# Two latent mixers reordered: rotation products first, keys copied by ScalarE, pooling products between the scores, rotary keys on 128 rows

## The reference

```
h = modulate(rms_norm(x, ffn1_norm[l]), sh1, sc1);  x = x + 0.5 * g1 * swiglu(h, ...)
h = modulate(rms_norm(x, mix_norm[l]), sh2, sc2)
z = h @ w_in[l]                       # 512 pooling, 384 query, 256 key/value, 64 rotary key
y_pool = (windowed means of z - z) @ pool_w[l], per group of 128, * pool_scale[l]
q = rms_norm(cq) @ w_q_b              # 4 heads of 128 plain + 64 rotary
k_nope, v = rms_norm(ckv) @ w_kv_b    # 4 heads of 128 and 128
q_rope, k_rope = apply_rope(...)      # x * cos + rotate_half(x) * sin; one k_rope for all heads
s = (q_nope . k_nope + q_rope . k_rope) * scale, causal, softmax over the keys, times v
x = x + g2 * (concat(y_pool, y_mla) @ w_out[l])
h = modulate(rms_norm(x, ffn2_norm[l]), sh3, sc3);  x = x + 0.5 * g3 * swiglu(h, ...)
```

## Time and profile before

| what | value |
|---|---|
| median of three executions | 1668.71 us (1668.25 to 1669.92) |
| profiled execution | 1669.04 us, of which the span is 1667.2 |
| mean granted TensorE clock | 0.985 |
| TensorE, its weight loads | 97% and 88% busy |
| VectorE, ScalarE, GpSimd | 76%, 51%, 4% busy |
| read from HBM | 340.6 MB, 205 GB/s |

### The profile page before, as it was taken

The page is one execution under the profiler, slowest core; times in us unless marked ns, Lnnn a source line. Parts: engine busy times, 40 slices in busy tenths (PEclk is TensorE's granted clock), DMA queues, the critical chain, the costliest instruction groups (busy, mean ns, idle before and its releaser), DMA issues.

```text
span 1667.2 us, 26979 instructions
## 1 busy us (share of the span) xinstructions
PE 1620.5 (97%) x11054; PEld 1461.2 (88%) x11054; DVE 1265.9 (76%) x1445; ACT 854.7 (51%) x1018; POOL 64.3 (4%) x77
## 2 busy tenths in 40 slices
PE   6999999999999999999999999999999999999997
PEld 6989999888689999899998799998899998799996
DVE  7967889877548897778878677885778887585554
ACT  4566555555256455554446464444544455454443
POOL 3001000000010000100000010000000000000000
PEclk8999999999799999999999999999999999999998
DMA  7514888654226986488874348975598844155550
GB/s 241 177 51 152 304 324 291 215 158 134 70 78 237 322 292 205 128 303 303 314 232 130 108 148 296 315 250 177 170 321 311 310 157 149 64 187 192 181 186 40
DMA packets 230974, 342.77 MB, mean 206 GB/s; under 512 B 7030, under 2 KB 194020, under 8 KB 230896
## 3 DMA queue, kind: packets, MB, share of 16 engines
q1 hardware_dynamic: 229888, 340.59, 60.3%
q0 software_dynamic: 704, 0.82, 0.2%
q10 hardware_dynamic: 304, 0.27, 0.1%
HBM read 340.60 MB, written 1.05 MB: 205 GB/s over the span
## 4 chain that ended last, share of the span: by engine, by line
PE 79%; DVE 11%; issue 5%; ACT 4%; POOL 0%; DMA 0%; DVEq 0%; ACTq 0%
PE PS L647 20%; PE PS L737 19%; PE PS L648 10%; PE PS L627 10%; PE PS L605 5%; DVE wl L1446 3%; PE PS L614 3%; PE PS L716 2%; PE PS L672 2%; ACT wh L1043 2%; PE PS L795 2%; PE PS L864 2%; DVE Z L1545 1%; PE PS L817 1%; DVE XL L1462 1%
## 5 line engine op out<-in xcount | busy, mean ns | idle before, releaser
L1446 DVE TENSOR_TENSOR wl<-raw,wh 128x2048 fp32r<-128x2048 f32 (+2 forms) x257 | 575.0, 2240 | 150.0 <-ACT wh L1043 147.9
L647 PE MATMUL PS<-HP,wh 128*128 128x512 f32 x1728 | 608.1, 395 | 0.2 <-DVE wl L1446 0.2
L1043 ACT ACTIVATE wh<-raw 128x2048 fp32r<-128x2048 f32 (+2 forms) x257 | 477.4, 1859 | 137.5 <-PE PS L737 117.9
L648 PE MATMUL PS<-HP,wl 128*128 128x256 f32 x1728 | 484.6, 280 | 0.0
L647 PEld LDWEIGHTS PS<-HP,wh 128*128 128x128 f32 x1728 | 324.0, 188 | 74.8 <-DVE wl L1446 0.5
L737 PE MATMUL PS<-FX,wh 128*128 128x256 f32 x1920 | 344.8, 281 | 1.9 <-DVE FX L1611 1.9
L648 PEld LDWEIGHTS PS<-HP,wl 128*128 128x128 f32 x1728 | 326.5, 189 | 0.0
L737 PEld LDWEIGHTS PS<-FX,wh 128*128 128x128 f32 x1920 | 294.5, 188 | 4.3 <-DVE wl L1446 2.1
L737 PE MATMUL PS<-FX,wl 128*128 128x256 f32 x960 | 269.9, 281 | 0.0
L737 PEld LDWEIGHTS PS<-FX,wl 128*128 128x128 f32 x960 | 180.4, 188 | 0.0
L1545 DVE SCALAR_TENSOR_TENSOR Z<-ada,CA,Z 128x1024 f32 x126 | 161.4, 1281 | 1.3
(11 more groups left out here) (263 smaller groups left out, 1796.9 us busy)
## 6 DMA issues: line engine op xcount, KB each, us to landing
ada<-ada_w SPq DMA_DIRECT2D x144, 512.0 KB, 6.3
raw<-ffn_w_gate SPq DMA_DIRECT2D x66, 1024.0 KB, 5.4
raw<-ffn_w_up SPq DMA_DIRECT2D x66, 1024.0 KB, 5.4
raw<-ffn_w_down SPq DMA_DIRECT2D x66, 1024.0 KB, 5.2
raw<-od_w_in SPq DMA_DIRECT2D x13, 1024.0 KB, 5.3
raw<-ev_w_in SPq DMA_DIRECT2D x10, 1024.0 KB, 7.9
raw<-w_in SPq DMA_DIRECT2D x8, 1024.0 KB, 5.5
raw<-w_out SPq DMA_DIRECT2D x8, 1024.0 KB, 6.1
```

What stands on the lines that cost most here:

```text
L647: mm(pairs(bank(bk)), lhsT=lhs(0, k), rhs=HP[:, k], start=k == 0, stop=False, skip_group_check=True)
L648: last = mm(bank(bk, 0, S), lhsT=lhs(1, k), rhs=HH[:, k, :], start=False, stop=k == k_tiles - 1, skip_group_check=True)
L1043: last = A_(dst(wh), src, ACT.Copy)
L1446: last = tt(dst(wl), src, dst(wh).bitcast(F32), ALU.subtract)
```

## The change

TensorE: the rotation group moves in front of `ada_turn` and the values' products, and `ada_turn` goes to bank 2. The pooling products move behind `scores(0)`, into banks 6 and 7. `spin(8)` and `spin(6, 6)` are left out, and the wait for `y_pool` moves behind `turn(1)`. VectorE: the rotary sums move in front of the adaptive columns; the rotary key is written into two tiles, KR with the key on partitions 0 to 63 and KX with it on 64 to 127, the other half of each zero, in place of one tile with the key doubled; the copy of the plain keys leaves VectorE; the pooling scale moves behind `masked(0)`, the `fill` behind `probs(0)`, and `lo(n0 + 10)` behind `masked(1)`. ScalarE: it gets the copy of the plain keys, in front of the values' copies, and `exps(0)` moves in front of the `fill`. GpSimd: it zeroes the other halves of KR and KX once the rotation group is through. The rotary scores now take all 128 partitions of the query tile, which holds two heads, against KR for even and KX for odd heads. The number of score products is the same.

```diff
@@ -417,8 +417,7 @@
                     half = slice(64 * (h % 2), 64 * (h % 2) + 64)
                     sc.append((h * w, [
                         (Z[:, ML["QN"] + h * S + b * P:][:, 0:P], Z[:, ML["KN"] + h * S:][:, 0:w]),
-                        (Z[half, ML["QR"] + (h // 2) * S + b * P:ML["QR"] + (h // 2) * S + (b + 1) * P],
-                         Z[half, ML["KR"]:ML["KR"] + w])]))
+                        (Z[:, ML["QR"] + (h // 2) * S + b * P:][:, 0:P], Z[:, ML[("KR", "KX")[h % 2]]:][:, 0:w])]))
                     va.append((bank((0, 3)[b], h * P, P),
                                [(Z[:, ML["V"] + kb * 512 + h * P:][:, 0:P], h * nk + kb) for kb in range(nk)]))
                 sc.sort(key=lambda e: (e[0] // w) % 2)
@@ -571,6 +570,12 @@
                         pool.tensor_tensor(sq[:, 2 * c, :], sq[:, 2 * c, :], sq[:, 2 * c + 1, :],
                                            ALU.add).then_inc(sq_sum, 1)
 
+            def zero_keys(l):
+
+                pool.wait_ge(ev("rot_full"), l + 1)
+                pool.memset(Z[64:P, ML["KR"]:ML["KR"] + S], 0.0).then_inc(ev("kr_zero"), 1)
+                pool.memset(Z[0:64, ML["KX"]:ML["KX"] + S], 0.0).then_inc(ev("kr_zero"), 1)
+
             for name in ("mix0", "ffn0", "mix1"):
                 add_squares(name)
             pool.wait_ge(ev("lru_gates"), 4)
@@ -579,9 +584,13 @@
             pool.dma_start(AR[0:12, 0:NSEL], const[0:12, NCONST:NCONST + NSEL]).then_inc(sel_in, 16)
             for name in ("ffn1", "fa0", "w0"):
                 add_squares(name)
+            zero_keys(0)
             pool.wait_ge(ev("pool_full"), 1)
             pool.dma_start(PW[:], A["pool_w_2"][1].rearrange("g c d -> c g d")).then_inc(aux_in[2], 16)
-            for name in ("fb0", "fa1", "w1", "fb1", "final"):
+            for name in ("fb0", "fa1", "w1"):
+                add_squares(name)
+            zero_keys(1)
+            for name in ("fb1", "final"):
                 add_squares(name)
 
         @block.tensor
@@ -972,41 +981,38 @@
                     last = product(bank(3 + h // 2, (h % 2) * S, S), lambda p, k: w(p, k, 256 * h, P),
                                    lambda p, k: H[p][:, 3 + k, :], 2)
                 last.then_inc(ev("kn_full"), 1)
-                ada_turn(f"w{l}", 6)
+                pe.wait_ge(ev("q_out"), 3 * l + 3)
+                mm(bank(6), lhsT=cn("rot"), rhs=Z[:, ML["QR"]:ML["QR"] + 512], start=True, stop=True)
+                mm(bank(0, 0, S), lhsT=cn("krdup", 64), rhs=Z[0:64, ML["KX"]:ML["KX"] + S], start=True, stop=True)
+                mm(bank(0, S, S), lhsT=cn("krrot", 64), rhs=Z[0:64, ML["KX"]:ML["KX"] + S], start=True,
+                   stop=True).then_inc(ev("rot_full"), 1)
+                ada_turn(f"w{l}", 2)
                 for b in range(NB):
                     last = product(bank(5 + 2 * b), lambda p, k: H[p][:, 3 + k, b * P:(b + 1) * P],
                                    lambda p, k: w(p, k, 0, 1024).rearrange("p (h c) -> p h c", c=256)[:, :, 128:256], 2)
                 last.then_inc(w_used, 1)
 
-                pe.wait_ge(ev("q_out"), 3 * l + 3)
-                pe.wait_ge(ada_out, ADA[f"w{l}"] + ADA_GAP[f"w{l}"])
-                mm(bank(6), lhsT=cn("rot"), rhs=Z[:, ML["QR"]:ML["QR"] + 512], start=True, stop=True)
-                mm(bank(0, 0, S), lhsT=cn("krdup", 64), rhs=Z[0:64, ML["KX"]:ML["KX"] + S], start=True, stop=True)
-                mm(bank(0, S, S), lhsT=cn("krrot", 64), rhs=Z[0:64, ML["KX"]:ML["KX"] + S], start=True,
-                   stop=True).then_inc(ev("rot_full"), 1)
-
+                rounds = latent_rounds()
+                scores, turn, values = attend("mla", l, rounds)
+                pe.wait_ge(ev("rope"), 2 * l + 2)
+                pe.wait_ge(ev("kn_out"), l + 1)
+                scores(0)
+                pe.wait_ge(ev("v_out"), 2 * l + 2)
                 pe.wait_ge(aux_in[1 + l], 16)
                 pe.wait_ge(ev("pool_diff"), 4 * l + 4)
                 for g in range(4):
-                    last = mm(bank(1 + g // 2, (g % 2) * S, S), lhsT=PW[:, g, :],
+                    last = mm(bank(6 + g // 2, (g % 2) * S, S), lhsT=PW[:, g, :],
                               rhs=cols(WK, 2176, 4)[:, g, :], start=True, stop=True)
                 last.then_inc(ev("pool_full"), 1)
-                rounds = latent_rounds()
-                scores, turn, values = attend("mla", l, rounds)
-                pe.wait_ge(ev("v_out"), 2 * l + 2)
-                spin(8)
-                pe.wait_ge(ev("rope"), l + 1)
-                pe.wait_ge(ev("kn_out"), l + 1)
+                pe.wait_ge(ada_out, ADA[f"w{l}"] + ADA_GAP[f"w{l}"])
                 n0, fill = U0[f"w_out{l}"], f"yw{l}"
-                scores(0)
-                spin(6, 6)
-                pe.wait_ge(ev("y_pool"), 4 * l + 4)
                 scores(1)
                 turn(0)
                 half_unit(n0, 4, fill, False)
                 values(0)
                 half_unit(n0 + 1, 5, fill, False)
                 turn(1)
+                pe.wait_ge(ev("y_pool"), 4 * l + 4)
                 spin(3, 7)
                 values(1)
                 half_unit(n0 + 2, 6, fill, False)
@@ -1395,6 +1401,8 @@
                 A_(Z[:, ML["QN"] + 512:ML["QN"] + 1024], bank(2), ACT.Copy).then_inc(ev("q_out"), 1)
                 A_(Z[:, ML["QR"]:ML["QR"] + 512], bank(1), ACT.Copy).then_inc(ev("q_out"), 1)
                 hi(nq + 4)
+                act.wait_ge(ev("kn_full"), l + 1)
+                A_(Z[:, ML["KN"]:ML["KN"] + 1024], banks(3, 2), ACT.Copy).then_inc(ev("kn_out"), 1)
                 act.wait_ge(w_used, nq + 3)
                 for b in range(NB):
                     A_(Z[:, ML["V"] + 512 * b:][:, 0:512], bank(5 + 2 * b), ACT.Copy).then_inc(ev("v_out"), 1)
@@ -1413,8 +1421,8 @@
                     else:
                         act.wait_ge(ev("mla_taken"), 2 * l + 2)
 
+                exps(0)
                 fill((0, 1), ready)
-                exps(0)
                 turned(0)
                 exps(1)
                 turned(1)
@@ -2013,32 +2021,27 @@
                         ALU.mult, ALU.subtract).then_inc(ev("pool_diff"), 1)
                 lo(n0 + 9)
 
-                ada_read(f"w{l}")
+                QR, t2 = Z[:, ML["QR"]:ML["QR"] + 512], WK[:, 0:512]
+                dve.wait_ge(ev("rot_full"), l + 1)
+                dve.wait_ge(ev("pool_diff"), 4 * l + 4)
+                dve.wait_ge(ev("tables"), 2)
+                own.mark(tt(pairs(t2), pairs(bank(6)), over(SIN[:], 2), ALU.mult))
+                own.mark(tt(pairs(QR), pairs(QR), over(COS[:], 2), ALU.mult))
+                own.mark(tt(WK[:, 512:768], bank(0, S, S), SIN[:], ALU.mult))
+                own.link(tt(WK[:, 768:1024], bank(0, 0, S), COS[:], ALU.mult))
+                own.mark(tt(QR, QR, t2, ALU.add))
+                dve.wait_ge(ev("kr_zero"), 2 * l + 2)
+                for h, name in ((0, "KR"), (64, "KX")):
+                    last = tt(Z[h:h + 64, ML[name]:ML[name] + S], WK[h:h + 64, 768:1024], WK[h:h + 64, 512:768], ALU.add)
+                    last.then_inc(ev("rope"), 1)
+
+                ada_read(f"w{l}", 2)
                 dve.wait_ge(ada_out, ADA[f"w{l}"] + ADA_GAP[f"w{l}"])
                 gain_cols(l, 2)
                 half_cols(l, 1)
                 shift_cols(1, 0 if l == 0 else 2)
                 if l == 0:
                     gain_cols(1, 0)
-
-                QR, t2 = Z[:, ML["QR"]:ML["QR"] + 512], WK[:, 0:512]
-                KR = Z[:, ML["KR"]:ML["KR"] + S]
-                dve.wait_ge(ev("rot_full"), l + 1)
-                dve.wait_ge(ev("pool_diff"), 4 * l + 4)
-                dve.wait_ge(ev("tables"), 2)
-                own.mark(tt(pairs(t2), pairs(bank(6)), over(SIN[:], 2), ALU.mult))
-                own.mark(tt(pairs(QR), pairs(QR), over(COS[:], 2), ALU.mult))
-                own.mark(tt(WK[:, 512:768], bank(0, S, S), SIN[:], ALU.mult))
-                own.link(tt(KR, bank(0, 0, S), COS[:], ALU.mult))
-                own.mark(tt(QR, QR, t2, ALU.add))
-                tt(KR, KR, WK[:, 512:768], ALU.add).then_inc(ev("rope"), 1)
-                dve.wait_ge(ev("kn_full"), l + 1)
-                dve.tensor_copy(Z[:, ML["KN"]:ML["KN"] + 1024], banks(3, 2)).then_inc(ev("kn_out"), 1)
-                lo(n0 + 10)
-                dve.wait_ge(ev("pool_full"), l + 1)
-                for g in range(4):
-                    last = ts(T[:, g, :], bank(1 + g // 2, (g % 2) * S, S), pc(f"ps{l}", g), None, ALU.mult)
-                    last.then_inc(ev("y_pool"), 1)
                 rounds = latent_rounds()
                 masked, probs = attention("mla", l, rounds)
                 def ready(c):
@@ -2048,9 +2051,14 @@
                         dve.wait_ge(ev("mla_taken"), 2 * l + 2)
 
                 masked(0)
+                dve.wait_ge(ev("pool_full"), l + 1)
+                for g in range(4):
+                    last = ts(T[:, g, :], bank(6 + g // 2, (g % 2) * S, S), pc(f"ps{l}", g), None, ALU.mult)
```

(4 more changed lines are left out.)

## The result

The changed kernel took 1656.51 us (median of five, 1649.87 to 1657.67) beside 1668.71 (median of five, 1665.93 to 1669.92). In a later comparison the same pair gave 1656.83 beside 1670.19, ratio 0.9915 [0.9893, 0.9938]. It is faster by 12 to 13 us, under 1%; 1654 was forecast, with a range of 1651.5 to 1660, so the gain was 12 where 15 had been forecast. The profiled execution took 1656.51 us with a span of 1654.4, 12.8 less than before.

A forecast was written before the change was run, and what follows sets the result against it. TensorE was taken to bound the kernel (79% of the span's last-ending chain). Per layer 4.07 + 3.1 - 0.43 = 6.74 us; two layers plus 1.7 for the clock give 15.2, so 1669.0 becomes 1653.8, say 1654; range 1651.5 to 1660.

The forecast's parts named there:

- Step 1: Latent mixer, keys' products to first scores: earlier rotation and keys' copy on ScalarE start the scores 4.07 us sooner per layer.
- Step 2: Latent mixer's score rounds: 128 rows throughout end the alternation price of 0.2 us per product, 3.1 us per layer gained.
- row-packing rule: Latent scores: products with few rows run side by side, so padding would cost about 0.4 + 0.9 us per layer.
- Step 3: Between the score rounds: six fillers (1.3 us) leave the path, pooling products (1.73) enter; net +0.43 us per layer.
- Step 4: VectorE's queue up to the second probabilities: ready at 947.2, TensorE wants them at 947.35, a slack of 0.15 us.
- Rival (b): Latent mixer: VectorE's queue sets the pace, 1 to 1.5 us lost per layer, 1656 to 1657.5 us; chance 0.15.
- the dearer load: ScalarE's table load at 2.66 us with draining: first probabilities 1.2 us late per layer, time about 1656.4 us.
- Step 5: Behind the second turning: order unchanged, lead kept; the later weight load lands at 951.3, hidden with 12 us to spare.
- rival (d): Feed-forward stage behind the mixer: paced by its loads, it gives the lead back; no change, 1669 us; chance 0.04.
- The sum: Both layers: 6.74 us each plus 1.7 for layer 1's clock fall not recurring, 15.2 us in all.
- rivals a: New stages without fillers: one or two stretches at 1.2 GHz, 1.7 or 3.3 us, 1655.6 to 1657.4 us; chance 0.17.
- Rival (e): Attention part of both layers: TensorE loses its clock without fillers, 14.4 us more per layer, 1683 us; chance 0.03.

The follow-up runs named there:

- late rotation: The changed kernel with the rotation products behind the values' products again; 1661.99 us, or 1663.59 us with 14 filler products in TensorE's wait.
- 64-row run: The changed kernel with the rotary scores on 64 rows again, everything else kept; 1659.21 us.
- grouped order: The changed kernel with rotary scores on 64 rows, each round as four plain products, then rotary of even heads, pause, rotary of odd heads; 1657.1 us.
- 128 rows alone: The kernel before with only the rotary scores on 128 rows, the two key tiles, their zeroing and the seventh rotary instruction; 1664.08 us.

## Why the prediction was right, and by how much each term was off

- **Step 1** (4.07 us): measured 9.93 - 5.96 = 3.97. The rotary sums began 2.45 us behind the start that marks the end of the keys' products, in place of 2.29. No engine was later: that start is 927.09 by the timeline and 927.16 by the chain that the prediction used (0.07), and it comes 0.12 us behind the start of the last keys' product now, where it came 0.21 behind it before (0.09). The keys' copy took 1.02 and was hidden. The zeroing took two times 0.31 and was hidden; the upper end of 2.04 for it was far off. The runs with the keys on VectorE and the late rotation price the two parts at 1.3 and 3.1 us, each by itself; the two don't add up to 3.97 exactly, since each is what the first scores lose with the other part in place.
- **Step 2** (3.1 us): the mechanism was right, the size was not. The rounds give 2.5 (3.43 + 5.04 - 2.21 - 3.78), the 64-row run 2.67. The mis-sized term is the pause in the middle of a round: it was put at 0.1 in all and is 0.32 in each round. Before, slow products hid most of it: the start behind it came 0.33 us after the last one where 0.21 was usual, now 0.33 where 0.11 is. The row-packing rule of the Trainium skill (TensorE: Matmul & The Clock Gate, "Part 3: Packing small matmuls") predicted a loss from padding, and the runs show a gain. They don't test the rule itself: a 128-row product, or in the grouped order the pause, stood between any two 64-row products of different halves.
- **Step 3** (0.43 us lost): right, the pooling products take 1.73 on the path.
- **Step 4**: VectorE was in time, with 0.6 us of slack in place of 0.15, because TensorE came 0.6 us later than forecast and VectorE 0.1. Rival (b) was near: one misplaced split makes it true, and without the pauses 0.2 is left. The table load took 1.28 and the exponentials then waited for VectorE (0.26), not for a drain; the dearer load of the Trainium skill (ScalarE: Activation LUTs, "What ACT_TABLE_LOAD costs") isn't seen here either.
- **Step 5**: right. The load issued at 939.10 before goes at 946.46 and nobody waits for it. A weight conversion of ScalarE that began at 992.24 began at 986.64 (5.60 earlier), one at 1397.47 at 1391.65 (5.82), one at 1456.93 at 1443.30 (13.63). Nothing was given back in the feed-forward stages, so rival (d) is out.
- **The sum**: 6.08 in layer 0 and 7.73 in layer 1, 13.8 in place of 15.2. The spans differ by 12.8; 0.5 is lost by the later end of the keys' products in layer 0 and 0.8 behind 1594 us, in the last part of the kernel, and 0.3 is gained between the two mixers. What makes up the 0.8 is not shown. Of the 1.4 between the two sums, twice 0.6 is step 2's and twice 0.1 step 1's.
- **The clock** (rivals a and e): turned round. The forecast feared for the new stages; they kept 1.00 in every one of the 16 passes whose order is that of the changed kernel (two profiles of it and six with small edits), while the kernel before lost it in three of four. Rival (e) named a real mechanism: the late rotation loses 2.8 us per layer to the clock when its wait of 3.55 us is left idle, and nothing when it is filled. It failed because the change shortens the wait to 0.35 us, so there was nothing to fill. The 1.7 us that the sum counted for the clock is what one pass of the kernel before lost; in its second profile both lost, and there the stretches are 9.2 and 13.8 us longer than now. So the size of that term is an accident of the one profile that the prediction read. The total shows no such gain either: the second pair of profiles, 1671.49 and 1656.68, is 14.8 us apart, since that execution of the kernel before came to layer 0's mixer 7.7 us earlier than the changed kernel's.

What stays open is what exactly made the kernel before fall. Its wait was short (0.74 us). With 128-row scores and a wait of 1.30 us (128 rows alone) or 1.70 us (keys by VectorE) the clock didn't fall, and with 64-row scores and a wait of 0.35 us it didn't either. Both together seem to be needed, but two passes each don't show it. Not tested by themselves were three parts of the new order: the exponentials ahead of the rounding of T, the pooling products behind the first scores, and the small adaptive columns behind the rotary sums.

## What to carry to other kernels

Count the waits of TensorE and the changes of row count between products, not only products: padding a short operand with zeros was worth 2.7 us per 16 products, 0.17 each, and grouping by row count gave three quarters of that. A part of such a change can be worth next to nothing alone (0.66 us) and 2.7 with the right order on the other engines, so look at what ends the next wait before you judge it. And measure a change of 1% in the stretch that it touches, between two instructions of one trace: here that repeated to 0.02 us where the total scattered by 7. Look at the granted clock of the stretch first, and take a second profile of the kernel before: its stretch differed by up to 7.7 us between passes.

## What was not expected of the hardware

A wait of TensorE for its own earlier product cost 0.32 us each time at full pace (0.22 ahead of the next start and 0.10 behind it), by the changed kernel with and without it. After 3.55 us of idling TensorE ran at the 1.2 GHz level in both layers (0.91 over 40 us), and 14 products of zeros prevented it both times. Zeroing 64x256 on GpSimd took 0.31 us both times; the first ran beside VectorE's split of a unit, which took 2.29 us as before, and the second beside a rotary product that reads PSUM, which took 0.68 (before 0.69).
